# The output projection of a two-layer decoder trunk, written as seven block products instead of eight

## What is computed

```python
merged = jax.nn.sigmoid(gate_a) * y_a + jax.nn.sigmoid(gate_b) * y_b
x = x + g1 * (merged @ w_out[l])
h = rms_norm(x, norm2_g[l]) * (1.0 + sc2) + sh2
x = x + g2 * ((jax.nn.silu(h @ w_gate[l]) * (h @ w_up[l])) @ w_down[l])
```

## Time and profile before

| | us |
|---|---|
| median of the runs | 2895.96 |
| the profiled execution's own time | 2895.48 |
| its span, first to last instruction | 2893.6 |
| TensorE busy in the span | 2829.5 |
| VectorE busy | 2103.5 |
| GpSimd busy | 1253.3 |
| ScalarE busy | 1223.9 |

### The profile page before, as it was taken

One profiled execution on the slowest core, in us unless ns is written; L12 is line 12 of the kernel. 1 busy time (PEld: TensorE's weight loads), 2 busy tenths in 40 slices (PEclk: granted clock), 3 DMA queues, 4 the chain that ended last, 5 costly groups with the idle time before them and its releaser, 6 DMA issues.

```text
span 2893.6 us, 38026 instructions
## 1 busy us (share of the span) xinstructions
PE 2829.5 (98%) x13924; PEld 2386.9 (82%) x13924; DVE 2103.5 (73%) x2575; ACT 1223.9 (42%) x1965; POOL 1253.3 (43%) x834
## 2 busy tenths in 40 slices
PE   6999999999999999999999999999999899999998
PEld 6888889988877888888878888898888788888887
DVE  7998688865687777757668896788533878776665
ACT  3433377762242333344542335778313333233443
POOL 0354322242535555554625452223223555555454
PEclk9999999999999999999999999999999999999999
DMA  7565400224615544466635652011351345544665
GB/s 293 166 195 177 152 16 13 51 50 155 223 51 192 169 170 164 153 199 217 198 131 160 186 177 74 17 23 41 106 175 44 122 158 174 180 163 155 196 196 167
DMA packets 332745, 408.59 MB, mean 141 GB/s; under 512 B 52369, under 2 KB 242961, under 8 KB 328338
## 3 DMA queue, kind: packets, MB, share of 16 engines
q1 hardware_dynamic: 290128, 298.41, 34.0%
q10 hardware_dynamic: 42434, 107.77, 10.0%
HBM read 299.33 MB, written 104.40 MB: 140 GB/s over the span
## 4 chain that ended last, share of the span: by engine, by line
PE 86%; DVE 6%; ACT 3%; DMA 2%; POOL 1%; issue 1%; SPq 0%; ACTq 0%; DVEq 0%; POOLq 0%
PE ps L709 15%; PE ps L711 15%; PE ps L712 15%; PE ps L1775 9%; PE ps L1777 9%; PE ps L1776 9%; PE ps L1635 4%; PE ps L1616 2%; PE ps L1656 2%; PE ps L1655 2%; PE ps L1621 2%; PE ps L1620 2%; DMA raw<-in_w_b_out 1%; DVE h_lo L2581 1%; DMA ada_rows<-in_w_ada 1%
## 5 line engine op out<-in xcount | busy, mean ns | idle before, releaser
L655 POOL TENSOR_TENSOR wlo<-blocks,whi 128x512 fp32r<-128x512 f32 x288 | 430.3, 1501 | 378.0 <-ACT whi L649 375.2
L693 POOL TENSOR_TENSOR wlo<-raw,whi 128x1024 fp32r<-128x1024 f32 (+4 forms) x156 | 236.4, 1532 | 706.3 <-ACT whi L685 706.2
L649 ACT ACTIVATE whi<-blocks 128x512 fp32r<-128x512 f32 x288 | 180.4, 627 | 316.9 <-PE ps L1777 254.1
L2441 DVE TENSOR_TENSOR d_hi_lo<-blocks,d_hi_lo 128x512 fp32r<-128x512 f32 x154 | 204.3, 1330 | 140.7 <-ACT d_hi_lo L1912 140.4
L666 POOL TENSOR_TENSOR d_hi_lo<-w_pair,d_hi_lo 128x512 fp32r<-128x512 f32 x148 | 203.4, 1377 | 199.4 <-ACT d_hi_lo L1912 199.4
L709 PE MATMUL ps<-h_hi,whi 128*128 128x512 f32 x832 | 281.6, 401 | 7.0 <-DVE h_lo L2581 5.5
L711 PE MATMUL ps<-h_lo,whi 128*128 128x512 f32 x832 | 274.5, 393 | 0.0
L712 PE MATMUL ps<-h_hi,wlo 128*128 128x512 f32 x832 | 273.4, 391 | 0.0
L685 ACT ACTIVATE whi<-raw 128x1024 fp32r<-128x1024 f32 (+4 forms) x162 | 106.9, 699 | 353.0 <-PE ps L712 292.3
L1775 PE MATMUL ps<-h_hi,whi 128*128 128x512 f32 x640 | 249.5, 390 | 5.3 <-issue 3.2
L1777 PE MATMUL ps<-h_hi,wlo 128*128 128x512 f32 x640 | 249.1, 389 | 0.0
(11 more groups left out here) (338 smaller groups left out, 6888.4 us busy)
## 6 DMA issues: line engine op xcount, KB each, us to landing
blocks<-hidden_scratch SPq DMA_DIRECT2D x154, 256.0 KB, 3.7
ada_raw<-in_w_ada SPq DMA_DIRECT2D x64, 512.0 KB, 4.2
raw<-in_w_in SPq DMA_DIRECT2D x92, 256.0 KB, 4.6
w_pair<-in_w_down SPq DMA_DIRECT2D x22, 1024.0 KB, 6.2
sums_scratch<-w_pair ACTq DMA_DIRECT2D x22, 1024.0 KB, 3.9
w_pair<-sums_scratch SPq DMA_DIRECT2D x88, 256.0 KB, 3.3
blocks<-in_w_gate SPq DMA_DIRECT2D x84, 256.0 KB, 3.2
blocks<-in_w_up SPq DMA_DIRECT2D x84, 256.0 KB, 3.0
```

The costliest lines, as they stand in the source:

```text
L649: act.activation(block_view(whi, s), blocks[:, r, :], ACT.Copy).then_inc(block_hi.sem, 1)
L655: pool.tensor_tensor(block_view(wlo, s), blocks[:, r, :], block_view(whi, s).bitcast(F32), ALU.subtract)\
L693: last = pool.tensor_tensor(dst(wlo[:, s, :]), src(raw[:, s, :]), dst(whi[:, s, :].bitcast(F32)), ALU.subtract)
L2441: return dve.tensor_tensor(out, value, hi.bitcast(F32), ALU.subtract)
```

## The change

The eight units of the output projection become 28 **steps** (`out_step`), 7 products x 4 steps, numbered 0 to 27 here, of 12 matmuls each. Operands go through rings of three places, as in the down projection. The products P1, P6, P2, P7, P4, P5, P3 come in this order; P1, P2, P5 and P3 use banks 0-3, the others banks 4-7. The weight sums (`first_sums`, `second_sum`, `last_sum`) and the activations' sums (`mg_raw`) are made by VectorE, partly during the merge. VectorE adds products into `uo_part` and `x_sb` in 36 instructions of 512 columns, placed behind given steps (`out_evictions`). Banks are handed over one by one: step 16 (the first of P4) and step 24 (the first of P3) wait before each of their four columns for that column's eviction, and so does `first_up`.

The first token half of `x_sb` is complete after P4 (step 19). Its mean of squares stands behind step 21, two products ahead of the end of the projection, `norm_scale` behind step 22. GpSimd adds up only the squares of tiles 0 to 3; those of tiles 4 to 7 are summed by TensorE (`summed_squares`), in both halves. The 16 `w_ada` products and their loads move from the projection to layer 0's down projection (one every third step from step 6; `next_c` is loaded once the last feed-forward product is done). The two Fori loops of the merge are unrolled, and `w_out` is loaded as four whole row pairs of 1 MB during the merge.

```diff
+    OUT = ("P1", "P6", "P2", "P7", "P4", "P5", "P3")
...
-                for n in range(KT - 2):
-                    unit_ready(pe, l, U_OUT + n)
-                    wait(pe, wo_ev, l, n - 1)
-                    for k in range(KT):
...
+                def out_step(n):
+
+                    p, j = divmod(n, OPAIRS)
+                    name = OUT[p]
+                    if j == 0:
+                        if name in ("P1", "P6"):
+                            wait(pe, mg_free, l, KT - 1 + (name == "P6"))
...
+                        elif name in ("P7", "P5"):
+                            pe.wait_ge(wo_ev.sem, wo_ev.at(l, 4 if name == "P7" else 20))
+                    pe.wait_ge(wo_lo_w.sem, wo_lo_w.at(l, n + 1))
+                    if n < OPAIRS:
+                        pe.wait_ge(mg_ready.sem, mg_ready.at(l, n + 1))
+                    else:
+                        pe.wait_ge(wo_lo_h.sem, wo_lo_h.at(l, n - OPAIRS + 1))
+                    for m in range(4):
+                        if j == 0 and name in ("P4", "P3"):
+                            pe.wait_ge(wo_ev.sem, wo_ev.at(l, (15 if name == "P4" else 29) + m))
+                        end = out_product(n, m)
...
+                def summed_squares(l, o):
+
+                    half = o % 2
+                    wait(pe, sq_added[half], l, (KT - 1) * (o // 2) + 3)
+                    for t in range(4):
+                        at = 4 * half + t
+                        pe.matmul(ps[:, 6, at:at + 1], sq_sum[:, at * P:(at + 1) * P], mean_col[:, :],
+                                  start=(t == 0), stop=False, skip_group_check=True)
+                    for k in range(4, KT):
+                        wait(pe, sq_ready[half], l, KT * (o // 2) + k + 1)
+                        for t in range(4):
+                            at = 4 * half + t
+                            last = pe.matmul(ps[:, 6, at:at + 1], square_view(o // 2, half, k)[:, t * P:(t + 1) * P],
+                                             mean_col[:, :], start=False, stop=(k == KT - 1), skip_group_check=True)
...
+                for n in range(OSTEPS):
+                    out_step(n)
+                    if n == 21:
+                        pe.wait_ge(wo_ev.sem, wo_ev.at(l, 28))
+                        summed_squares(l, 2)
+                    if n == 22:
+                        norm_scale(l, 2)
...
+                for n in range(OPAIRS, OSTEPS - 1):
+                    if n == 17:
+                        for m in (0, 1):
+                            part_added(m, 4)
+                    if n == 24:
+                        norm_inverse(l, 2)
+                    if n == 25:
+                        for m in (0, 1):
+                            fifth_out(m)
+                    out_hidden_low(n)
+                    for j in {9: (0,), 13: (1,), 21: (2, 3)}.get(n, ()):
+                        last_sum(j)
+                    out_evictions(n)
...
+                    if l + 1 < DEPTH and n >= ADA_STEPS and n % 3 == 0 and n < ADA_STEPS + 6 * KT:
+                        at = (n - ADA_STEPS) // 3
...
+                        ada_product(l, 4 * KT + at, at // KT, next_raw, next_c)
```

More of the change, by code:

```diff
@@ L143, in trunk @@
     U_MERGE = 34
-    U_OUT = 42
-    U_FFN = 50
+    U_FFN = 42
     UNITS = U_FFN + 2
@@ L1727, in _ @@
                     end[1].then_inc(unit_used.sem, 1)
-                for n in range(KT - 2):
-                    unit_ready(pe, l, U_OUT + n)
-                    wait(pe, wo_ev, l, n - 1)
-                    for k in range(KT):
-                        if n == 0:
-                            wait(pe, mg_ready, l, KT if k == KT - 1 else KT - 1)
-                        end = tile_products(pe, n % 2, 2 * (n % 2), mg_hi, mg_lo, [(k, k)],
-                                            first=(k == 0), last=(k == KT - 1))
-                    end[1].then_inc(unit_used.sem, 1)
@@ L1739, in last_out @@
-                def last_out(n, t, ks):
-                    for k in ks:
-                        last = tile_half(pe, n % 2, 2 * (n % 2) + t, t, mg_hi, mg_lo, k, k == 0, k == KT - 1)
-                    return last
-                for n in (KT - 2, KT - 1):
-                    unit_ready(pe, l, U_OUT + n)
-                    wait(pe, wo_ev, l, n - 1)
-                    last_out(n, 0, range(KT)).then_inc(out_half.sem, 1)
-                last_out(KT - 2, 1, range(5))
-                mean_squares(l, 2)
@@ L1750, in _, with out_product @@
-                last_out(KT - 2, 1, range(5, KT)).then_inc(unit_used.sem, 1)
-                norm_scale(l, 2)
-                last_out(KT - 1, 1, range(KT)).then_inc(unit_used.sem, 1)
+                def out_product(n, m):
+                    p, j = divmod(n, OPAIRS)
+                    name, col = OUT[p], slice(m * P, (m + 1) * P)
+                    return products(pe, [ps[:, D_BANK[name] + m, :]], ow_tile(n, 0)[:, col], ow_tile(n, 1)[:, col],
+                                    [(oh_tile(n, 0), oh_tile(n, 1))], j == 0 and name in D_OPENS, j == OPAIRS - 1,
+                                    name not in D_OPENS)[0]
```

436 lines of the change are left out of this document (302 added, 134 removed).

## The result

The changed kernel takes 2936.97 us (median of 4 runs, 2935.73 to 2938.09) against 2896.21 of the kernel before on the same chip (4 runs, 2895.23 to 2897.43): 1.014 times, 95% interval 1.0123 to 1.0158. It is slower by 41 us; 2894.1 had been predicted. Its profiled execution has a span of 2936.3 us.

A forecast was written before the change was run, and what follows sets the result against it. TensorE, busy 98%, bounds the projection; behind it, when the second half's `norm_scale` is reached. Fixed part -11.6, waits +9.2, moved work +1.0: -1.4 us on 2895.48, so 2894.1 us; own range 2889 to 2899, 8 in 10 for 2886 to 2903.

The forecast's parts named there:

- Matmuls removed: Output projection: 336 matmuls instead of 384 in each layer, 48 fewer at 0.227 us, -10.88 us a layer.
- Steps 4 and 16: Projection: TensorE waits for VectorE, 1.3 us before step 4 (0 to 2.5), 1.5 at step 16 (0 to 2.6).
- Behind step 21: Projection: TensorE waits 1.0 us for P4's evictions, with VectorE about 0.9 us late (0.1 to 2.5).
- Clock: Behind step 21: granted clock may halve after waits and one-column matmuls, 0.6 us a layer (0 to 1.3).
- price of a one-column matmul: Each token half gets 16 more at 0.20 us; in the first half they add 3.25 us on TensorE's path.
- Second half: From the projection's last matmul to `norm_scale` 11.54 us instead of 9.69: +1.85 us a layer (0 to 2.5).
- Moved work: Layer 0's down projection: moved `w_ada` products and loads cost 1.0 us once (0 to 3).
- SyncE, held at step 2 ... 0.2: Layer 0's down steps: SyncE held until the last feed-forward product issues step 3's loads late, costing 0.2 us.
- VectorE becomes the bound: Slower rival: VectorE over 2.6 us late at steps 12 to 15 or 19 to 21; 2903.7 us, chance 0.18.
- The lock counts in full: Slower rival: each GpSimd collision costs VectorE 1.29 us, 0.32 more, +2.2 us a layer; 2898.5 us, chance 0.12.
- What would prove it wrong: VectorE's gaps closing at steps 12 to 22, projection waits under 1 or over 8 us a layer, clock staying down.

The follow-up runs named there:

- Experiment 5: The changed kernel with VectorE's four differences of the last product at steps 6 to 9 instead of 9, 13 and 21: 2929.13 us.
- Experiment 7: The changed kernel with VectorE's projection work in another order (seven changes), first half's one-column matmuls behind step 23, row product behind 24: 2912.91 us.
- Experiment 2: The changed kernel with 11 of the first half's 20 one-column matmuls left out: 2927.33 us.
- experiment 6: The changed kernel with the second half's squares summed by GpSimd alone and four one-column matmuls later in the up projection: 2929.63 us.
- experiments 10: Experiment 7's kernel plus experiment 6's change, layer 0's moved modulation products at least three steps apart, last product's evictions ahead of VectorE's reciprocal: 2893.53 us.
- experiment 11: The kernel before with the first half's four one-column matmuls issued five times over (20), in both layers, nothing else: 2909.73 us.
- experiment 3: The changed kernel with the next layer's modulation work, including SyncE's wait, three steps later in the down phase: 2932.85 us.
- experiment 1: The changed kernel with the first half's one-column matmuls behind step 23 instead of 21, row product behind 24 instead of 22: 2941.63 us.
- experiment 12: The kernel of experiments 10 with GpSimd summing six first-half squares (12 one-column matmuls left), its first additions one step earlier, `uo_part` evictions at step 26: 2893.05 us.

## Why the prediction was wrong

*Matmuls removed: right.* 28 steps at 2.72 us where TensorE neither waited nor ran at half clock; -10.88 a layer came.

*Steps 4 and 16: right in place and cause, low in size.* 1.3 and 1.5 were said, 1.8 and 2.6 came; VectorE's stretch from step 12 to 15 drifted at 2.96 a step where 2.99 was said, so the drift wasn't too small. But step 16's own low part met a GpSimd instruction and took 1.78 us instead of 0.68: it ended 5.3 us after ScalarE's release (765.00) where 4.2 was said.

*"Behind step 21: 1.0 (0.1 with VectorE on time, 2.5 behind the 1024-column split)": the first step that failed.* 3.6 us came, and a wait of 2.0 before step 21 that no term had. I counted VectorE "about 0.9 late". The trace shows a VectorE and a GpSimd instruction taking turns at 1.70 to 1.74 us where the sum used 1.59, and in steps 19 to 21 GpSimd had two a step: 3.4 us in a step of 2.72. So GpSimd fell behind and never paused, and each of VectorE's instructions took a turn beside it. The low part of step 21 ended 7.3 us after ScalarE's release (781.18), 4.8 later than in a steady step. I had added collisions to VectorE one by one and never asked whether GpSimd's own row fitted into the step. The two last differences (2.87 and 0.68), queued ahead of the low part of step 22, weren't in this term at all. Experiment 5 separates the two: without the differences the wait behind step 21 shrinks to 2.35, and the one before it stays. Experiment 7 takes both away together.

*"Clock: 0.6, half of such a loss (0 to 1.3)": the step that cost most.* The rows that I had cited themselves hinted at it, and the earlier trace rows; I took a part of the smallest loss that they bore out. Another stretch of the same trace, which I had not looked at, shows it with no wait at all: 32 matmul rows of 128, 16 and one column, and then half clock:

```profile
327.47 1.93 PE L1540 MATMUL ps<-columns,lat_sq 128*128 128x1 f32 x16
```
```profile
327.00:329.30 2.30, 2.30 (x23) 2.30 (x22) 2.20 (x5) 0.00 (x0) 0.00 (x0) 1.00 0.66 239
329.40:332.70 3.30, 3.30 (x8) 2.57 (x9) 3.18 (x7) 0.00 (x0) 0.00 (x0) 0.50 0.16 35
```

In the changed kernel it came for 13.7 us: 4.5 on the one-column rows (8.55 instead of 4.06) and 2.4 on step 22. Experiment 2 shows it behind a wait; the changed kernel's second half (beside experiment 6) and experiments 10 and 11 show it without one. So the price of a one-column matmul, 0.20, was read rightly and was not the whole price: the 16 added matmuls, +3.25 in my sum, cost 5.9 us a layer in the kernel before, where nothing waits (experiment 11).

*Second half: +1.85 was said, +4.9 came.* From the projection's end to `norm_scale` it is 14.6 us, not 11.54: 1.5 for the half clock behind the columns (seven matmuls; thirteen in layer 1, where it was +5.6), 0.9 for the bank of the last eviction, which I had left out, and 0.5 on the columns themselves.

*Moved work: 1.0 (0 to 3) was said, 9.0 came.* "SyncE, held at step 2 ... 0.2" was the mis-sized term: 4.7 at steps 2 to 5, all of which went in experiment 3's trace when the same wait stood behind the loads of step 5. The products beside SBUF evictions cost 4.3 us at six steps, not 0.8 at one: a product of 1.22 takes 2.31 beside GpSimd.

```profile
1342.87 2.31 DVE L2581 CUSTOM_DVE_ANT_0 next_raw<-next_raw,next_c 128x1024 f32<-128x1024 f32 x1
```

*The rivals.* "VectorE becomes the bound" had the right mechanism and its point of decision was met (2.7 us late at the low part of step 16, 4.8 at step 21), but of the upper ends in its 9.4 a layer those behind step 21 (2.5 for 3.6) and of the clock (1.3 for 6.9) were too low, and step 21 had none; layer 0 lost 21.3 in the projection, 3.25 of them foreseen. "The lock counts in full" asked for 1.29 + 0.68 = 1.97 us a pair; 1.70 to 1.74 came, between that and my 1.59, and nearer to mine. The Trainium skill (SBUF — State Buffer, section "SBUF: two separate sides") says that the one that starts first has the shared port pair for its whole instruction. This trace shows the turns, but not the full sum. Instructions with one operand in PSUM take no turns: in the changed kernel's trace 131 such VectorE instructions of 512 columns lie beside a GpSimd one for over 95% of their time, and they take 0.67 to 0.74 us.

*What would prove it wrong* was named rightly: TensorE's waits above 8 us a layer (9.1 in layer 0), a granted clock that falls and stays down (13.7 us in each layer).

## What to carry to other kernels

Before work moves to fill idle engines, add up, step by step, what the two engines that share memory each have in that step at their price together (1.7 us a pair here), not over the whole: VectorE's mean of 73% said nothing of three steps in which GpSimd's row alone took 125% of the step. A short wait on TensorE is priced with what follows it at half clock, and so is a row of tiny matmuls. In queues that run in order, a wait belongs behind everything that the next two steps need; moving a consumer without its producers (experiment 1) only moves the wait.

## What the runs showed of the hardware

Forty one-column rows in a row, at 0.11 us each and with no wait ahead of them, left the granted clock at 0.50, the level of 1.2 GHz, for the next 9 to 12 matmuls in experiments 7, 10 and 11 and for 7 and 13 in the changed kernel's second halves. Twenty-four did so in experiment 12, in both layers. Eight with no wait ahead never did; eight behind a wait of 1.56 us did once in the changed kernel (rows at 1496.13, half clock from 1498.23).

Behind the 3.56 us wait of the changed kernel it stayed at half for 13.7 us, through all the one-column rows and step 22. Equal waits were not always followed by the same clock: the waits of some 2 us before steps 16 and 21 were followed by full clock in the changed kernel's layer 0, and by 3.4 us of half clock in experiments 3 and 6, whose projection is the same.
